# Gate bias added by VectorE, a transition by token tile, and S5 on array tiles, in a two-block fp32 kernel

## The reference

```
h = rms(x, g0) * (1 + scale_m) + shift_m          # ada: scale, shift, gate from silu(c) @ ada_w
o_a .. o_d = diff attention, mLSTM, GLA, S5       # each 256 x 512, from h @ w_in_2
merged = sum_i sigmoid(h @ w_gate[i] + b_gate[i]) * (o_i @ w_branch[i])      # i = 0..3
x = x + gate_m * rms(merged @ w_out, g1)
x = x + gate_f * rms(ffn(rms(x, g2) * (1 + scale_f) + shift_f), g3)
S5: bu = b_re u, b_im u (32 groups of 16 channels, 64 states); x_t = a x_(t-1) + bu_t; y = c_re x_re - c_im x_im + d u
```

## Time and profile before

| | us |
|---|---|
| median of 3 runs | 2720.89 (2720.29 to 9454.43) |
| profiled execution | 2721.06 |
| its span | 2719.3 |
| mean granted TensorE clock | 0.992 |
| busy: TensorE, VectorE, ScalarE | 2650.8 (97%), 1906.8 (70%), 1254.7 (46%) |
| chain that ended last | TensorE 86%, VectorE 6%, ScalarE 3%, DMA 2%, issue 2% |

### The profile page before, as it was taken

How to read it: one execution, slowest core, us unless ns; L and a number is a source line. 1 busy time by engine, 2 the same in 40 slices (tenths; PEclk the granted TensorE clock), 3 DMA queues, 4 the chain that set the end, 5 groups by cost and what they waited for, 6 DMA issues and landing times.

```text
span 2719.3 us, 36265 instructions
## 1 busy us (share of the span) xinstructions
PE 2650.8 (97%) x13230; PEld 2237.7 (82%) x13230; DVE 1906.8 (70%) x2275; ACT 1254.7 (46%) x1519; POOL 281.9 (10%) x322
## 2 busy tenths in 40 slices
PE   8999999999999998999999999999999999999997
PEld 8998888888888887898977788777778888888886
DVE  6777677788778777665686778687755555555687
ACT  5445544444444445455555444444554444444443
POOL 0040041324132000071000000000000000000000
PEclk9999999999999998999999999999999999999999
DMA  9646687788778885756554655588656656666784
GB/s 343 215 163 214 219 278 257 266 276 273 263 264 276 270 271 165 228 171 208 164 169 151 223 200 174 189 300 284 217 178 193 188 191 192 187 191 191 257 291 165
DMA packets 294705, 606.18 MB, mean 223 GB/s; under 512 B 25873, under 2 KB 26065, under 8 KB 292673
## 3 DMA queue, kind: packets, MB, share of 16 engines
q1 hardware_dynamic: 290272, 578.55, 64.8%
q0 software_dynamic: 4320, 26.13, 2.6%
HBM read 593.31 MB, written 11.29 MB: 222 GB/s over the span
## 4 chain that ended last, share of the span: by engine, by line
PE 86%; DVE 6%; ACT 3%; DMA 2%; issue 2%; POOL 0%; SPq 0%; DVEq 0%; ACTq 0%; POOLq 0%
PE ps L540 84%; DVE w_lo L1780 2%; ACT w_hi L1178 1%; DMA w_raw<-in_w_in 1%; DVE arena L1775 1%; PE ps L645 1%; DMA w_raw<-in_w_up 1%; DMA w_raw<-in_w_gate 0%; ACT arena L1209 0%; DVE x L1790 0%; PE ps L672 0%; PE ps L635 0%; DMA arena<-gain_scratch 0%; PE ps L656 0%; DVE arena L2375 0%
## 5 line engine op out<-in xcount | busy, mean ns | idle before, releaser
L1780 DVE TENSOR_TENSOR w_lo<-w_raw,w_hi 128x1024 fp32r<-128x1024 f32 x904 | 1127.0, 1250 | 765.0 <-ACT w_hi L1178 757.2
L1178 ACT ACTIVATE w_hi<-w_raw 128x1024 fp32r<-128x1024 f32 x904 | 951.1, 1054 | 1375.8 <-PE ps L540 1283.0
L540 PE MATMUL ps<-w_hi,hop_hi_part 128*128 128x512 f32 x2144 | 846.7, 395 | 8.1 <-issue 2.5
L540 PE MATMUL ps<-w_hi,hop_lo_part 128*128 128x512 f32 x2144 | 836.9, 390 | 0.0
L540 PE MATMUL ps<-w_lo,hop_hi_part 128*128 128x512 f32 x2144 | 836.8, 390 | 0.0
L540 PEld LDWEIGHTS ps<-w_hi,hop_hi_part 128*128 128x128 f32 x2144 | 403.9, 188 | 100.8 <-issue 13.4
L540 PEld LDWEIGHTS ps<-w_hi,hop_lo_part 128*128 128x128 f32 x2144 | 403.7, 188 | 85.1
L540 PEld LDWEIGHTS ps<-w_lo,hop_hi_part 128*128 128x128 f32 x2144 | 404.1, 188 | 81.6
L540 PE MATMUL ps<-w_hi,hid_hi_part 128*128 128x512 f32 x992 | 389.1, 392 | 2.8 <-DVE hid_lo_part L2447 1.5
L540 PE MATMUL ps<-w_hi,hid_lo_part 128*128 128x512 f32 x992 | 386.3, 389 | 0.0
L540 PE MATMUL ps<-w_lo,hid_hi_part 128*128 128x512 f32 x992 | 386.0, 389 | 0.0
(11 more groups left out here) (302 smaller groups left out, 1462.8 us busy)
## 6 DMA issues: line engine op xcount, KB each, us to landing
arena<-in_ada_w SPq DMA_DIRECT2D x256, 384.0 KB, 4.7
w_raw<-in_ffn_w_in SPq DMA_DIRECT2D x176, 512.0 KB, 3.5
w_raw<-in_w_in SPq DMA_DIRECT2D x152, 512.0 KB, 3.6
w_raw<-in_w_up SPq DMA_DIRECT2D x128, 512.0 KB, 3.9
w_raw<-in_w_down SPq DMA_DIRECT2D x128, 512.0 KB, 4.7
w_raw<-in_w_gate SPq DMA_DIRECT2D x128, 512.0 KB, 4.0
w_raw<-in_ffn_w_out SPq DMA_DIRECT2D x88, 512.0 KB, 3.6
w_raw<-in_w_out SPq DMA_DIRECT2D x64, 512.0 KB, 5.1
```

The source lines that it names most:

```text
L540: return nc.tensor.matmul(o, w, r, start=start, stop=stop, skip_group_check=True)
L1178: return nc.scalar.activation(o, i, ACT.Copy, scale=scale)
L1780: V.tensor_tensor(w_lo[:, j % LEAD, :, 0:cols], w_raw[:, j % RAW, :, 0:cols], w_hi[:, j % LEAD, :, 0:cols].bitcast(F32), ALU.subtract).the ...
```

## The change

Three parts.

The bias of a gate no longer goes through TensorE. SyncE loads the row once, broadcast to 128 partitions (one load of 128 x 512); VectorE adds it to set 0 while moving it to SBUF, in iteration 7, which now frees the set; ScalarE's sigmoid is in iteration 8, on SBUF in place; the multiplication of iteration 9 waits for it (`gate_sig`). The load of the row stands one weight load later in SyncE's list (ahead of q = 3 instead of 2), for the gate of the same ten instead of the next, and waits until the previous gate's additions are done.

The passage from MLP to second in projection gets the form of that from out projection to FFN, with shared helpers: units 16 to 19 whole, units 20 to 23 by token half, and the first four units of the projection too (`staggered_chunk`). The ada products of this stretch go one to each iteration. The first three chunks of the projection change their order of columns; how many units are of which kind stays.

S5's input matmuls use 64 rows (the half in which the tile's groups lie) instead of 128, alternating between upper and lower half; the output matmuls give 32 columns (`2 * S5_CH`) each, to partitions 0, 32, 64 and 96 of the bank, instead of four sums over all 128.

```diff
-ADA_TAIL = [k + k // 4 for k in range(KT)]
+ADA_TAIL = list(range(KT))
...
-            sp.wait_ge(sem["gate_bias"], g + 1)
-            row = a["b_gate_2"][0][g // 4:g // 4 + 1, part(g % 4)]
-            for at in (0, 32):
-                sp.dma_start(gate_raw[at:at + 1, :], row).then_inc(sem["gate_rows_in"], 16)
+            if g:
+                sp.wait_ge(drained[0], H_GATE + g + 1)
+            else:
+                sp.wait_ge(sem["g_z"], 1)
+            sp.dma_start(gate_row, a["b_gate_2"][0][g // 4, part(g % 4)].partition_broadcast(P)).then_inc(sem["gate_rows_in"], 16)
...
                 n, q = j // 10, j % 10
-                if q == 2 and 4 * i + n + 1 < GATES:
-                    load_gate_rows(4 * i + n + 1)
+                if q == 3 and 4 * i + n:
+                    load_gate_rows(4 * i + n)
                 w = w_gate[i, q] if q < UA else w_branch[i, q - UA]
                 load(R_GATE + 5 * i, j, w[:, :, n * COLS:(n + 1) * COLS])
...
-        down(R, 16, H + 3, 0, 1, MLP_SUPER, between=last_group)
...
+        for n in range(2):
+            token_chunk(R, 16 + UB * n, H + 3, n, hid_hi[:, 1], hid_lo[:, 1], UB, between=last_group)
+        for n in range(2):
+            pe.wait_ge(drained[n], H + 5)
         pe.wait_ge(sem["mod_ready"], G_IN2)
-        turn_scaled(5, 0)
+        for t in range(TT):
+            for q in range(STAGGER):
+                n, k = 2 + q // UB, q % UB
+                if t == 0:
+                    pe.wait_ge(sem["lo_ready"], R * 8 + (20 + q + 1))
+                elif q == 3:
+                    turn_half(5, 0, SCALED_TOK)
+                m = token_half(20 + q, n % 2, t, hid_hi[:, 1], hid_lo[:, 1], UK * k, k == 0, k == UB - 1)
+                if t == 1:
+                    m.then_inc(sem["unit_done"], 1)
+                elif k == UB - 1:
+                    m.then_inc(sem["half_done"], 1)
...
+        staggered_chunk(5, R_IN2, H_IN2, SCALED_TOK)
+        for c in range(1, 4):
+            chunk(R_IN2, UA * c, H_IN2 + c // 2, c % 2, ftiles=1 if c == 3 else FT, between=gain_steps)
...
-            for ii in range(4):
-                m = mm(PS[4 + ii // 2][:, (ii % 2) * S:(ii % 2 + 1) * S], span(S5_B[t % 2] + 2 * part, ii * P, P),
-                       T(40 + t), start=ii % 2 == 0)
+            for ii in (0, 2, 1, 3):
+                rows = slice(64 * (ii // 2), 64 * (ii // 2) + 64)
+                m = mm(PS[4 + ii // 2][:, (ii % 2) * S:(ii % 2 + 1) * S], span(S5_B[t % 2] + 2 * part, ii * P, P)[rows],
+                       T(40 + t)[rows], start=ii % 2 == 0)
             m.then_inc(sem["s_bu_psum"], 1)
...
-                m = mm(PS[6][:, 0:S], span(S5_C[t % 2] + 2 * part, ii * P, P), ROT[part][:, ii],
-                       start=part == 0 and ii == 0, stop=part == 1 and ii == 3)
+                own = 2 * S5_CH * ii
+                m = mm(PS[6][own:own + 2 * S5_CH, 0:S], span(S5_C[t % 2] + 2 * part, ii * P + own, 2 * S5_CH), ROT[part][:, ii],
+                       start=part == 0, stop=part == 1)
...
-                g = 4 * i + n
-                pe.wait_ge(drained[0], H + n + 1)
-                pe.wait_ge(sem["gate_bias"], g + 2)
-                for t in range(TT):
-                    mm(SETS[0][t][:], gate_ones[ROWS, :], gate_hi[ROWS, g % 2, :], stop=False)
-                for q in range(UA):
-                    token_unit(R, 10 * n + q, 0, hop_hi, hop_lo, UK * q, False, q == UA - 1)
-                    steps(10 * n + q)
+                token_chunk(R, 10 * n, H + n, 0, between=steps)
...
-                if j % 10 == 7:
+                if j % 10 == 8:
                     n = j // 10
...
-                    for t in range(TT):
-                        m = nc.scalar.activation(flat(o)[:, t * COLS:(t + 1) * COLS], SETS[0][t][:], ACT.Sigmoid)
-                    m.then_inc(drained[0], 1)
-                if j % 10 == 3 and 4 * i + j // 10 + 1 < GATES:
-                    gate_bias_hi(4 * i + j // 10 + 1)
+                    o = T(4, FT) if i else merged(n)
+                    act.wait_ge(drained[0], H_GATE + 4 * i + n + 2)
+                    nc.scalar.activation(o, o, ACT.Sigmoid).then_inc(sem["gate_sig"], 1)
...
+        last_part(2, 0)
+        last_part(3, 0)
+        pair_variance(3, 0)
+        last_part(2, 1)
+        pair_inverse(3, 0)
+        mid_scaled(0, half(0)).then_inc(sem["rows_ready"], 1)
+        split(R_IN2, 0)
+        for b in range(2):
+            turned_half(5, 0, b, gain5, 0)
+        lo_half(5, 0, 0)
+        last_part(3, 1)
+        split(R_IN2, 1)
+        lo_half(5, 0, 1)
...
+                if j % 10 == 7:
+                    n = j // 10
+                    sig = T(4, FT) if i else merged(n)
+                    dve.wait_ge(sem["gate_rows_in"], 16 * (4 * i + n + 1))
+                    dve.wait_ge(sem["unit_done"], R * 8 + (j + 1))
+                    if i == 0:
+                        dve.wait_ge(sem["x_parked"], 16)
+                    elif (i, n) == (1, 0):
+                        dve.wait_ge(sem["hid_ready"], MLP_SUPER + 2)
+                    else:
+                        dve.wait_ge(sem["sig_free"], 4 * (i - 1) + n)
+                    for t in range(TT):
+                        m = V.tensor_tensor(flat(sig)[:, t * COLS:(t + 1) * COLS], SETS[0][t][:], gate_row, ALU.add)
+                    m.then_inc(drained[0], 1)
                 if j % 10 == 9:
                     n = j // 10
                     sig = T(4, FT) if i else merged(n)
-                    dve.wait_ge(drained[0], H + (n + 2))
+                    dve.wait_ge(sem["gate_sig"], 4 * i + n + 1)
...
-                if j % 10 == 4 and 4 * i + j // 10 + 1 < GATES:
-                    gate_bias_lo(4 * i + j // 10 + 1)
```

More of the change, by code:

```diff
@@ L299, in two_blocks @@
     GATES = 4 * 4
[L300 to L303, removed]
+    gate_row = flat(row_store[:])
     def merged_tok(n):
@@ L815, in last_group @@
         def last_group(u):
-            if u == 21:
+            if u == 17:
                 modulation((G_MLP + MLP_SUPER // 2) * KT)
-        down(R, 16, H + 3, 0, 1, MLP_SUPER, between=last_group)
[L822 to L836, removed]
@@ L848, in gain_steps @@
                 pe.wait_ge(sem["gain_ready"], 1)
-                pe.wait_ge(sem["xT_ready"], TURNED[5] + 4)
+                pe.wait_ge(sem["xT_ready"], TURNED[5] + 10)
                 turn_gain(4)
[L852 to L857, removed]
+        staggered_chunk(5, R_IN2, H_IN2, SCALED_TOK)
+        for c in range(1, 4):
+            chunk(R_IN2, UA * c, H_IN2 + c // 2, c % 2, ftiles=1 if c == 3 else FT, between=gain_steps)
         modulation((G_IN2 + 1) * KT, 6)
@@ L1420, in _ @@
                 hidden_relu(1, H_MLP + 35, MLP_SUPER - 1)
-            if j in (18, 20, 22):
-                both_squares((j - 18) // 2)
-        def mid_rows(c):
-            turned_rows(5, c, lambda k: gain5[:, k:k + 1], lambda k: mod[:, k:k + 1])
-        both_squares(3).then_inc(sem["tok_sums"], 1)
-        token_guess(3, SUM_MID, 2)
-        mid_rows(0)
-        mid_rows(1)
+            if j == 18:
+                both_squares(0)
+        both_squares(1)
+        half_square(2, 0, 4)
+        half_square(3, 0, 8).then_inc(sem["tok_sums"], 1)
+        pair_guess(3, 0)
+        split(R_IN2, 0)
+        half_square(2, 1, 24)
+        split(R_IN2, 1)
+        hi_half(5, 0, 0)
+        hi_half(5, 0, 1)
+        half_square(3, 1, 28).then_inc(sem["tok_sums"], 1)
+        hi_half(5, 0, 2)
+        hi_half(5, 0, 3)
+        pair_guess(4, 1)
+        split(R_IN2, 2)
+        split(R_IN2, 3)
+        for b in range(STAGGER):
+            hi_half(5, 1, b)
+        rest_rows(5, 2, gain5, 0)
         def narrow_wait(c, q):
@@ L2124, in _ @@
                 for t in range(TT):
-                    m = V.tensor_tensor(Y_TOK[:, t, part(n)], x_tok[:, t, part(n)], wide[:, part(n)], ALU.mult)
-                m.then_inc(sem["rows_ready"], 1)
-        mid, both = (tok_var[:, TT * i:TT * (i + 1)] for i in (SUM_MID, SUM_Y))
-        dve.wait_ge(sem["tok_sums"], 3)
-        V.reduce_sum(mid, sums[:, SUM_MID], axis=AX_X)
-        then(V.reduce_sum(both, sums[:, SUM_Y], axis=AX_X))
-        V.tensor_scalar(both, both, 1.0 / D, None, ALU.mult)
@@ L2134, in _, with last_part @@
-        then(V.tensor_scalar(mid, mid, 1.0 / D, EPS, ALU.mult, ALU.add))
-        stt(both, mid, EPS, both, ALU.mult, ALU.add).then_inc(sem["tok_var"], 1)
-        token_inverse(3, SUM_MID, 2)
-        scale_rows(SCALED_TOK, Y_TOK, SUM_Y)
-        for b in range(4):
-            lo_pair(5, b)
+                    m = gained(t, n)
+                m.then_inc(sem["mid_gained"], 1)
+        def last_part(n, t):
+            k = 2 * t + n - 2
+            if t == 0:
+                dve.wait_ge(sem["half_done"], n - 1)
+            else:
+                dve.wait_ge(sem["unit_done"], (R_MLP + 29) * 8 + 20 + UB * (n - 1))
+            V.tensor_tensor(x_tok[:, t, part(n)], SETS[n % 2][t][:], x_tok[:, t, part(n)], ALU.add).then_inc(sem["mid_added"], 1)
```

(39 more changed lines are left out.)

260 lines of the change are left out of this document (126 added, 134 removed).

## The result

The changed kernel takes 2752.2 us (2748.67 to 2754.13, 4 runs), the one before 2721.78 in the same job: ratio 1.011, 95% interval 1.0095 to 1.0125. That is 30 us slower; 2713 was forecast, and the range ended at 2732. One of the four runs of the kernel before took 9454.43 us; without it the median is 2720.89.

The account below looks back on a forecast made before the run. TensorE was taken to bound the kernel, with VectorE close under it. From 2721.06 us, -13.8 - 10.8 - 3.5 + 14 + 3 + 3 = -8.1 gave 2713.0, range 2691 to 2732.

Parts of the forecast that it names:

- 20 us in its sum: Gates: time given back through VectorE's delays, +14 S5 products, +3 clock, +3 GLA stage 0.
- TensorE's work, -13.8 and -10.8: Gates: removing 33-row bias matmuls saves 0.86 us in each of 16; S5 array tiles save 3.7 on inputs, 7.1 on products.
- the bounds' other end: S5 array tiles: saving only 0.4 us instead of 10.8, if no column tiles run at once.
- rival C: S5 products: column tiles don't overlap, each product takes 2.14 instead of 0.84 us, +10.4, 2723 us; chance 0.17.
- The passage, -3.5: MLP to second in projection: saves 3.5 us, bounds -4.6 and 0, with a new wait before unit 20.
- The S5 products, +14: The two S5 stages: late weight load delays VectorE 3.3 us per ten units, TensorE's products wait 12.0, with iteration 7 +14.
- Rival B: Gates: burst lands in 5.3 to 5.7 us, TensorE stands at products and gates' starts; 2729 us, chance 0.17.
- The rest of the waits, +3 and 0: Stage 0: GLA steps wait 1 us at each of three delays, +3; stage 3: few VectorE results awaited, 0.
- The clock, +3: S5 stages: granted clock falls behind two new waits, 1.4 us lost at each, +3.
- The forecast's own upper bound for what is given back, 30: S5 products: 3.3 us of delay at eight products, nothing regained, with the clock.
- Its lower end: Whole kernel: 2691 us, from 2697 with delays swallowed (chance 0.23), less the clock's 3 and a transition of -5.

Follow-up runs that it names:

- the passage alone: Kernel before the change, with only the passage from MLP to second in projection changed: 2719.55 us, ratio 0.9991.
- the wait alone: Kernel with two bias-row buffers, row sent at once, SyncE then waiting for the previous gate's additions ahead of load 10n+3: 2729.0 us, ratio 1.0019.
- the row at 10n+7: Changed kernel with SyncE's load of the bias row ahead of weight load 10n+7 instead of 10n+3: 2708.36 us, ratio 0.9946.
- two buffers: Changed kernel with two alternating bias-row buffers, the row waiting only for the additions of the gate before the last: 2706.92 us, ratio 0.9947.

## Why the prediction was wrong

The sign was wrong. It named the right mechanism (row behind its wait, late weight loads, VectorE behind, TensorE standing) and mis-sized what that gives back: 20 us in its sum, 55.5 in the traces. By its terms:

- *TensorE's work, -13.8 and -10.8.* The tiles: -10.8 forecast, 11.2 to 12 less measured; the bounds' other end, column tiles in series (rival C), is refuted. The 33-row matmuls are gone; what they were worth shows bare only in gates 13 to 16, 4.5 us in four gates (forecast 3.4), where no S5 step stands.
- *The passage, -3.5*: 2.4 by the ratio for the passage alone. Up to the gain transpose it is 3.8 in that trace and 4.8 in the changed kernel's. The new wait ahead of unit 20 was 2.13 us, of 2.5 allowed.
- *The S5 products, +14: the step that failed first.* "the load lands 3.7 later at the median plus 0.7 for the row ahead: U+8.4", so 4.4 behind the additions. It landed 6.35 behind them at the first product, 5.9 behind its issue. A median of loads issued one by one was carried over to a load at the head of a burst of five transfers. Rival B had nearly this price, 5.3 to 5.7, from the bytes and the rate of the profile. The waits for steps 12 and 15 rose by 19.7 (23.1 + 3.0 over 5.4 + 1.0), with one of 7.9 where the sum had at most 5.2 (the 2.19 of before and 3.0).
- *The rest of the waits, +3 and 0.* GLA's are 9.2, of which I had 3. Stage 3 was priced at nothing ("TensorE waits for few VectorE results"), but the ada sums (4.2) and the matmuls that need the additions' banks (2.4) wait on the same VectorE there: 4.6 us slower where 3.4 should have been saved. With the wait alone it is as before (127.1), and with the row at 10n+7 the saving is there (122.8).
- *The clock, +3: the term that was furthest off.* It is 18.3 more. I counted 1.4 us at two new waits; aligned with the wait it is 1.7 each, and there were thirteen waits of 1.87 us or more, eleven of them with a stretch of low clock behind. This and the products' waits are about as large.

Rival B was nearest: the burst lands nearly as it said, and TensorE stood for the additions (3.3 us, "over 3"). Its time, 2729, was still 23 short, since it took the clock at two waits more instead of at each, left stage 3 out and stage 0 at the forecast's 3. The forecast's own upper bound for what is given back, 30, counted eight products; the range should have had every stage and every wait's clock in it. (Its lower end has a slip that changes nothing: 2697 less 3 and less the 1.5 between a passage of -5 and one of -3.5 is 2692.5, not 2691.)

What is shown: the queue's wait, with nothing else changed, makes 22 us, and the row in the burst 23 more (two buffers, wait alone, changed kernel); and all of it goes with the row's place. The split between standing and clock is bookkeeping from one trace each and not an experiment, since no run could hold the clock up; but it closes to within 1 us for the change as a whole, for the wait and for the row. Which property of the burst makes its first load late (the row's bytes, the number of transfers, the spread over partitions) stays open: no run varied one of them alone.

Why the bias by VectorE saves nothing in stage 0, even with the row at 10n+7, the traces do show. Five gates should give 4.3 us up to gate 5. TensorE has 2.7 us of waits for GLA steps there, which the kernel before doesn't have, and behind the longer of them, 2.2, the clock falls:

```profile
1422.00:1427.00 5.00, 4.85 (x25) 4.03 (x26) 3.71 (x7) 1.06 (x1) 0.00 (x0) 0.66 0.67 214
```

That is 1.7 us more, 4.4 together.

## What to carry to other kernels

A wait put into a queue of prefetches is priced by everything behind it: find when the queue reaches it, when the awaited work is done, and how many loads then leave at once; price the first of these by the burst's bytes over the rate, not by the median landing (here the first gave 5.3 to 5.7 and the second 4.4, where 6.35 was measured). Put such a load where the queue arrives after its condition, or give it a second buffer; here one digit was worth 44 us. And work moved from the engine that bounds to one with 80% load saved only where little on the critical path waited for that engine (here in stage 3). Its place in the iteration mattered too: behind the step that others want it stood in less of TensorE's way than ahead of it, at the same length.

## What the runs showed of the hardware

Four fp32 matmuls on column tiles of 32 ran as fast as one of them would by the old price (eight records in 0.78 us, 0.37 beyond the 0.41 that going into and out of a shape cost elsewhere, against 2 x 0.214 for one), though all four read the same 128 rows. By the Trainium skill, TensorE: Matmul & The Clock Gate, Part 3, weight loads overlap matmuls only when the row group differs; this trace disagrees for column tiles of one row group, where the eight weight loads take 0.16 us in all, beside matmuls of 0.64. The table in the same part of that page of the Trainium skill has a speedup of 2.38 for three column tiles; here four tiles gave 2.2 for the whole call (1.73 over 0.78).

A row of 2 KB broadcast to 128 partitions, 256 KB written, took 3.3 to 7.4 us to land, 4.2 at the median. Three weight loads behind one landed 5.7, 6.5 and 8.5 us after their issue (least, middle, most), against 4.2, 5.1 and 5.9 for three without it.

The granted clock was 0.58 over the first 4 us behind a wait of 7.94 us, and 0.57 behind one of 2.19: the long one cost no more of it than the short one, 1.7 us either way, so that several short waits cost more clock than one long one. Not every wait did it: of the thirteen from 1.87 us up in the gates of the changed kernel, two (2.15 us from 1757.14, 2.03 from 1826.29) had the clock at 1.00 over the 8 us from their start.
